# RWKV stage: four groups of two heads in one block, the next group's first exponentials inside the scan, masks and spread products moved

## The chip, the cores and the metric

The kernel runs on one core of a Trainium2 chip. The metric is the device time of one execution in microseconds; where several runs were taken, their median. All times of single instructions come from one profiled execution.

The engines are named as in the profile: PE is TensorE (matmul), PEld its weight load, DVE is VectorE, ACT is ScalarE, POOL is GpSimd, and SP issues the DMAs and clears semaphores.

## The reference

One layer of a hybrid network on 1024 image tokens and 128 prompt tokens (1152 columns in all): an adaptive RMS norm and a half-step SwiGLU, a mixer, another half-step SwiGLU and a last norm. The mixer has a Fourier half and a half of eight RWKV-7 heads of size 64, read forward and backward. What concerns us is the RWKV half:

```python
def step(state, inp):
    r_t, w_t, k_t, v_t, kk_t, a_t = inp
    sa = jnp.einsum('bhvk,bhk->bhv', state, -kk_t)
    state = (state * w_t[:, :, None, :]
             + sa[..., None] * (kk_t * a_t)[:, :, None, :]
             + v_t[..., None] * k_t[:, :, None, :])
    return state, jnp.einsum('bhvk,bhk->bhv', state, r_t)
...
decay = jnp.exp(-jnp.exp(-jax.nn.softplus(-w_raw) - 0.5))
...
y_gn = ((y_sum - mean) * lax.rsqrt(var + GN_EPS)) * ln_w + ln_b
y_rwkv = (y_gn + (bonuses[0] + bonuses[1])) * gate
```

The step runs over all tokens for each head and direction; `y_gn` normalises over the 64 channels of a head, and `gate` is a small product with `gate_g2`.

## The kernel before

The program is a row of stages: load, modulation, first SwiGLU, input projection, Fourier, RWKV, output projection, second SwiGLU, final norm. A stage is a `Stage` object: it owns semaphores (`st.sem(...)`), runs one block in which each engine has its own program, and on leaving it runs one more block in which SP clears every semaphore of the stage, one instruction for each (`for s in self.sems: sp.sem_clear(s)`). All engines meet at the end of a block.

The RWKV part (`rwkv`) works on four groups of two heads. `rw_first` prepares group 0; then there is one stage per group (`rw_pair`: group 0, a hardware loop over groups 1 and 2, group 3); `rw_last` finishes the output of group 3. Both directions (d = 0 and 1) of a group are done together. The tokens are cut in 18 chunks of 64.

A group has two halves. The first one is the chunk algebra, all chunks at once:

- ACT makes two exponentials of each direction (`P0`, `iP0`, `P1`, `iP1`, lines 1979 and 1980; tiles `rw.e1`, `rw.e2`, which lie in the buffer `rw.gr`). DVE scales the operands with them (`pc`, `first`, `A`, `B`, `K`, `R`, lines 1802 to 1818). Ahead of these DVE adds the two directions' outputs of the group in front (`y`, line 1885; its second operand lies in `rw.work`).
- PE works through the list `jobs`, written out by hand; job n uses PSUM bank n % 8 and waits until job n-8 has been copied out. The names are `n` (the matrices to invert), `g` (twelve products, masked by DVE with `masked`, line 1832), `v` and `b` (transposes), `s` (states), `a`, `z`, `f`, `w`, `q`, `x`, `u`, `y`.
- The 16 x 16 diagonal blocks of `n` are inverted by DVE: ACT copies `n` to SBUF, SP sends it to DRAM (line 1532) and fetches its blocks back into lanes (line 1537, 8 DMAs for each direction), DVE does 15 elimination steps of two instructions each (`invert`, lines 1850 and 1853; semaphore steps `times` and `minus`), transposes them (`turn`, line 1857), and SP sends blocks back (lines 1542 and 1545, 8 DMAs each) and loads the whole matrices (`xt`, line 1548, and `x`, line 1550). Jobs `f` wait for `xt`.
- `share = [0, 3, 7, 11, 15]` tells where the masks of `g` jobs 8 to 11 stand between the elimination steps of direction 0: after 3, 7, 11 and 15 of them.
- In groups 1 to 3 (`done`) the norm of the group in front is woven in: jobs `mean`, `var`, `rstd` (the products that spread the reciprocal over the columns, line 1160, which wait for DVE's `inv` and `wide`, lines 1924 and 1167) and `gate`. `rstd` stands ahead of the `u` jobs of direction 0; on DVE `rstd` stands ahead of `rk0` and of the odd `u` jobs.

The second half is the scan, 18 steps. A step is two products on PE for each direction (`S`, line 1710, and `M`, line 1718) with a DVE instruction behind each (lines 1956 and 1965), and the output product `Y` (lines 1730 and 1735) of the step in front, which ACT copies out (line 2020). In groups 0 to 2 (`more`) the preparation of the next group (`Prep`) fills the gaps of the steps; its last instructions are three scans on DVE (line 1308). Preparation of `sw[0]`, which `P0` and `iP0` read, ends in step 11 of the scan.

Of the kernel before, what the change touches and what calls it, by code (L numbers as in the profile page):

```python
# [8 lines left out]
ALU = mybir.AluOpType  # L9
ACT = mybir.ActivationFunctionType  # L10
# [87 lines left out]
class Stage:  # L98


    def __init__(self, nc):
        self.nc, self.sems, self.ctx = nc, [], ExitStack()

    def sem(self, name):
        s = self.ctx.enter_context(self.nc.semaphore(name))
        self.sems.append(s)
        return s
# [988 lines left out]
class Rwkv:  # L1096
# [9 lines left out]
    def __init__(self, nc, ctx):  # L1106
# [31 lines left out]
        self.e1, self.e2 = [[g[:, n * T:(n + 1) * T] for n in (m, m + 1)] for m in (4, 6)]  # L1138
# [293 lines left out]
def rw_pair(nc, io, sb, rw, zd, md, nd, ud, utd, p, done, more):  # L1432
# [6 lines left out]

    GC, NU = 3, 6  # L1440
# [30 lines left out]
    jobs += post("var", 1) + many("g", 1, 6, 10) + many("x", 0, 0, NB) + many("g", 1, 10, G1) + post("rstd", NC)  # L1471
    jobs += many("u", 0, 0, 2 * NB) + many("f", 1, 0, NB) + many("z", 1, 0, NB) + many("y", 0, 0, NB) + post("gate", NC)
# [7 lines left out]
    share = [(BI - 1) * n // 4 for n in range(5)]  # L1480
# [3 lines left out]
    dve_names = ["y"] * done + ["pc0", "first0", "A0", "B0", "pc1", "first1", "A1", "B1", "K0", "R0"]  # L1484
# [3 lines left out]
    dve_names += ["t0"] + inv_of(1, 0, BI - 1) + ["t1", "K1", "R1"]  # L1488
    dve_names += names("mean", 0, 0, NC * done) + names("g", 1, 0, 2) + names("w", 0, 0, NB) + names("g", 1, 2, 6)
    dve_names += names("var", 0, 0, done) + names("g", 1, 6, 10) + names("x", 0, 0, NB) + names("g", 1, 10, G1)  # L1490
    dve_names += ["inv", "wide"] * done + names("rstd", 0, 0, NC * done) + ["rk0"] + odd(0) + names("bonus", 0, 0, NC * done)
# [5 lines left out]
    act_names += act_of("b", 1) + act_of("a", 1) + act_of("q", 1) + act_of("u", 1) + act_of("y", 1)  # L1497
    with Stage(nc) as st, nc.psum_tensor(fresh("g_ps"), [P, 8, 512], F32) as ps:
        pe_t = Steps(st.sem("pe_s"), [name(*job) for job in jobs])
        dve_t = Steps(st.sem("dve_s"), dve_names)  # L1500
        act_t = Steps(st.sem("act_s"), act_names)
        pool_t = Steps(st.sem("pool_s"), ["zero", "one"])
        n_out, n_in, u_out, u_in, t_out, t_in = ([st.sem(f"{n}{d}") for d in range(2)]
                                                 for n in ("n_out", "n_in", "u_out", "u_in", "t_out", "t_in"))
        y_out, s_in, g_in, out_s = st.sem("y_out"), st.sem("s_in"), st.sem("g_in"), st.sem("out_s")
        bank = {job: n % 8 for n, job in enumerate(jobs)}

        spe_t = Steps(st.sem("spe_s"), [x for i in range(NCH) for x in (f"S{i}_0", f"S{i}_1", *[f"Y{i - 1}"] * (i > 0), f"M{i}",
                                                                  *["st"] * (i == NPC + 1))] + [f"Y{NCH - 1}"])
        sdve_t = Steps(st.sem("sdve_s"), ["zero"] + [x for i in range(NCH) for x in  # L1510
                                                     [f"S{i}_0", f"S{i}_1"] + [f"M{i}_0", f"M{i}_1"]])
        sact_t = Steps(st.sem("sact_s"), [x for i in range(NCH) for x in [f"Y{i}"] + ["st"] * (i == NPC)])
        spool_t = Steps(st.sem("spool_s"), [f"mp{i}_{d}" for i, d in SD])
        prep = Prep(st, io, sb, rw, zd, p + 1, ps[:, 6:8, :]) if more else None

        def copied(eng, k, d, n):
            if on_act(k, d, n):
                act_t.wait(eng, name(k, d, n))
            if on_dve(k, d, n):
                dve_t.wait(eng, name(k, d, n))  # L1520

        with st.block() as block:
            @block.sync
            def _(sp):
                flat = lambda t, d: t[d][0:P * T].rearrange("(p t) -> p t", t=T)
                lanes = lambda t, h, b: t[(2 * h + b // 2) * NCH:(2 * h + b // 2 + 1) * NCH, b % 2]
                blocks = lambda t, h, b: diagonal(t, h)[b].rearrange("i c j -> c i j")
                HB = [(h, b) for h in range(2) for b in range(HS // BI)]

                def there(d):  # L1530
                    act_t.wait(sp, name("n", d, NB - 1))
                    sp.dma_start(flat(nd, d), work[:, d * T:(d + 1) * T]).then_inc(n_out[d], 16)
                    sp.wait_ge(n_out[d], 16)
                    if done:
                        dve_t.wait(sp, "y")
                    for h, b in HB:
                        sp.dma_start(lanes(ni[d], h, b), blocks(nd[d], h, b)).then_inc(n_in[d], 16)

                def back(d):
                    dve_t.wait(sp, f"minus{d}_{BI - 2}")  # L1540
                    for h, b in HB:
                        sp.dma_start(blocks(ud[d], h, b), lanes(wi[d], h, b)).then_inc(u_out[d], 16)
                    dve_t.wait(sp, f"t{d}")
                    for h, b in HB:
                        sp.dma_start(blocks(utd[d], h, b), lanes(wit[d], h, b)).then_inc(t_out[d], 16)
                    act_t.wait(sp, "iP1")
                    sp.wait_ge(t_out[d], 16 * len(HB))
                    sp.dma_start(xt[d].rearrange("p c n -> p (c n)"), flat(utd, d)).then_inc(t_in[d], 16)
                    sp.wait_ge(u_out[d], 16 * len(HB))
                    sp.dma_start(x[d].rearrange("p c n -> p (c n)"), flat(ud, d)).then_inc(u_in[d], 16)  # L1550

                for d, key in enumerate(("state_fwd", "state_bwd")):
                    sp.dma_start(rw.st[:, d, :], io[key][0, 0, bass.ds(p * 2, 2), :, :].rearrange("h v k -> (h v) k"))\
                      .then_inc(s_in, 16)
                there(0)
                there(1)
                back(0)
                back(1)
                if done:
                    pe_t.wait(sp, name("gate", 0, NC - 1))  # L1560
                sp.dma_start(rw.g2[:, :], io["gate_g2"][0][:, bass.ds(p * P, P)]).then_inc(g_in, 16)
                if done:
                    dve_t.wait(sp, name("gate", 0, NC - 1))
                    sp.dma_start(md[bass.ds(p + (NP - 1), 1), :, :].rearrange("a p t -> p (a t)"), y).then_inc(y_out, 16)
                if more:
                    pe_t.wait(sp, name("x", 1, NB - 1))
                    dve_t.wait(sp, name("rkk", 0, NC - 1))
                    prep.sync(sp)
                    for sem in prep.z_in + prep.w_in:
                        sp.wait_ge(sem, 16)  # L1570
                sact_t.wait(sp, "st")
                for d, key in enumerate(("state_f", "state_b")):
                    sp.dma_start(io[key][0, 0, bass.ds(p * 2, 2), :, :].rearrange("h v k -> (h v) k"), rw.m0[:, d, :])\
                      .then_inc(out_s, 16)
                for d in range(2):
                    sp.wait_ge(t_in[d], 16)
                    sp.wait_ge(u_in[d], 16)
                sp.wait_ge(s_in, 32)
                sp.wait_ge(g_in, 16)
                if done:  # L1580
                    sp.wait_ge(y_out, 16)
                sp.wait_ge(out_s, 32)

            @block.gpsimd
            def _(pool):
                both = work[0:LANES, 2 * T + 1024:2 * T + 2048]
                if done:
                    dve_t.wait(pool, "y")
                pool_t.did("zero", pool.memset(both, 0.0))
                pool_t.wait(pool, "zero")  # L1590
                pool_t.did("one", pool.memset(both.rearrange("p (k i) -> p k i", i=BI * BI)[:, :, ::BI + 1], 1.0))
                if done:
                    dve_t.wait(pool, "inv")
                    dve_t.wait(pool, "wide")
                for i, d in SD:
                    c = order[d][i]
                    if i:
                        sdve_t.wait(pool, f"M{i - 1}_{d}")
                    else:
                        sdve_t.wait(pool, "zero")  # L1600
                    spool_t.did(f"mp{i}_{d}", pool.tensor_scalar(rw.mp[:, d, :], old(i, d), rw.pc[:, d, c:c + 1], None, ALU.mult))

            @block.tensor
            def _(pe):
                def heads(out, q, w, v):

                    for j in range(NU):
                        for h in range(2):
# [4 lines left out]
                def pair(k, d, q, count, one):  # L1613

                    for j in range(count):
                        for h in range(2):
                            ins = one(ps[:, bank[k, d, 2 * q + h], :], rows_of[h], h, q * count + j, j)
                            if j == count - 1:
                                pe_t.did(name(k, d, 2 * q + h), ins)
# [532 lines left out]
```

## Time and profile before

| | |
|---|---|
| median of 3 runs | 3014.56 us (3010.67 to 3015.2) |
| the profiled execution, device time | 2998.61 us |
| its span (first to last instruction) | 2996.8 us |
| PE busy | 2674.4 us (89%) |
| DVE busy | 1360.5 us (45%) |
| ACT busy | 728.4 us (24%) |
| mean granted TensorE clock | 0.925 |
| RWKV groups, start of the first exponential's table load | 1383.38, 1519.15, 1656.54, 1805.13 us |
| first instruction of `rw_last` | 1934.08 us |

The profile's busy times are sums over the span, so they say which engine is loaded, not what a stage waits for. Granted clock 1.0 is 2.4 GHz and 0.5 is 1.2 GHz.

### The profile page before, as it was taken

To read this page: it belongs to the slowest core of one execution; us is meant where nothing else is said; L and a number is where in the kernel's file an instruction comes from. 1 tells how busy PE (TensorE), PEld (TensorE's weight loads), DVE (VectorE), ACT (ScalarE), POOL (GpSimd) and SP (SyncE) were. 2 spreads that over 40 slices of the span, in tenths; PEclk is the share of its full clock that TensorE was granted. 3 is DMA by queue.
4 is the path that set the end of the run, shared out by engine and by line. 5 is a ranking of instruction groups with operands and counts; after the bars stand their busy time and mean duration, and the time that the engine had idled before them with its cause. 6 is when DMAs were issued, how large, how long until landed. Compare 5 with 4: busy or idle time off the path is not lost. (4 is left out here: it accounts for less than half of the span.)

```text
span 2996.8 us, 51466 instructions
## 1 busy us (share of the span) xinstructions
PE 2674.4 (89%) x21152; PEld 2514.1 (84%) x21152; DVE 1360.5 (45%) x2687; ACT 728.4 (24%) x1367; POOL 86.9 (3%) x158
## 2 busy tenths in 40 slices
PE   4589999999999599976979697977899999999995
PEld 2189999999999599944867676777899999999995
DVE  1353333333333766316475757434533333333335
ACT  1141111111111411115444344222411111111112
POOL 0000000000000000000112020200000000000000
PEclk7689999999999799986889788988899999999997
DMA  8611111111110122142121212051111111111101
GB/s 340 262 50 43 42 42 42 42 42 42 42 42 7 29 84 90 50 175 79 50 62 38 62 37 62 12 183 36 50 43 42 42 42 42 42 42 42 42 7 63
DMA packets 213154, 193.64 MB, mean 65 GB/s; under 512 B 63860, under 2 KB 183455, under 8 KB 213023
## 3 DMA queue, kind: packets, MB, share of 16 engines
q1 hardware_dynamic: 212752, 191.65, 19.8%
q8 instruction: 101, 1.65, 0.2%
q14 instruction: 31, 0.25, 0.0%
q10 hardware_dynamic: 270, 0.09, 0.0%
HBM read 159.01 MB, written 32.70 MB: 64 GB/s over the span
## 5 line engine op out<-in xcount | busy, mean ns | idle before, releaser
L128 PE MATMUL ff_ps<-h_hi,ff_wlo 128*128 128x384 f32 x2112 | 711.1, 337 | 7.2 <-ACT ff_s L604 7.2
L129 PE MATMUL ff_ps<-h_lo,ff_whi 128*128 128x384 f32 x2112 | 710.2, 336 | 0.0
L130 PE MATMUL ff_ps<-h_hi,ff_whi 128*128 128x384 f32 x2112 | 709.6, 336 | 0.0
L652 DVE TENSOR_TENSOR ff_s<-ff_ps,ff_s 128x384 f32<-128x384 f32 x132 | 73.6, 557 | 752.2 <-PE ff_ps L130 750.9
L128 PEld LDWEIGHTS ff_ps<-h_hi,ff_wlo 128*128 128x128 f32 x2112 | 400.3, 190 | 7.8 <-ACT ff_s L604 7.8
L129 PEld LDWEIGHTS ff_ps<-h_lo,ff_whi 128*128 128x128 f32 x2112 | 400.0, 189 | 0.0
L130 PEld LDWEIGHTS ff_ps<-h_hi,ff_whi 128*128 128x128 f32 x2112 | 400.0, 189 | 0.0
L130 PE MATMUL ff_ps<-ff_uhi,ff_whi 128*128 128x384 f32 x1056 | 352.7, 334 | 0.0
L128 PE MATMUL ff_ps<-ff_uhi,ff_wlo 128*128 128x384 f32 x1056 | 352.7, 334 | 0.0
L129 PE MATMUL ff_ps<-ff_ulo,ff_whi 128*128 128x384 f32 x1056 | 352.7, 334 | 0.0
L604 ACT ACTIVATE ff_s<-ff_ps 128x384 f32<-128x384 f32 x132 | 65.0, 493 | 740.6 <-PE ff_ps L130 740.5
L608 ACT ACTIVATE ff_uhi<-ff_s 128x384 fp32r<-128x384 f32 x132 | 69.5, 526 | 556.2 <-DVE ff_s L652 556.2
L663 DVE SCALAR_TENSOR_TENSOR x_again<-ff_ps,mod,x_again 128x256 f32<-128x256 f32 (+1 forms) x352 | 171.0, 514 | 72.1 <-PE ff_ps L130 71.4
L663 DVE SCALAR_TENSOR_TENSOR x<-ff_ps,mod,x 128x256 f32<-128x256 f32 (+1 forms) x352 | 170.9, 514 | 72.2 <-PE ff_ps L130 71.5
L128 PEld LDWEIGHTS ff_ps<-ff_uhi,ff_wlo 128*128 128x128 f32 x1056 | 198.2, 188 | 0.0
L129 PEld LDWEIGHTS ff_ps<-ff_ulo,ff_whi 128*128 128x128 f32 x1056 | 198.2, 188 | 0.0
L130 PEld LDWEIGHTS ff_ps<-ff_uhi,ff_whi 128*128 128x128 f32 x1056 | 198.2, 188 | 0.0
L645 DVE TENSOR_TENSOR ff_wlo<-ff_raw,ff_whi 128x1024 fp32r<-128x1024 f32 x132 | 157.5, 1219 | 17.7 <-ACT ff_whi L599 17.5
L128 PE MATMUL pj_ps<-h_hi,pj_wlo 128*128 128x384 f32 x456 | 154.1, 338 | 1.6 <-DVE h_lo L466 1.6
L129 PE MATMUL pj_ps<-h_lo,pj_whi 128*128 128x384 f32 x456 | 153.1, 336 | 0.0
L130 PE MATMUL pj_ps<-h_hi,pj_whi 128*128 128x384 f32 x456 | 153.1, 336 | 0.0
L599 ACT ACTIVATE ff_whi<-ff_raw 128x1024 fp32r<-128x1024 f32 x132 | 131.9, 1044 | 0.0
(287 smaller groups left out, 3247.9 us busy)
## 6 DMA issues: line engine op xcount, KB each, us to landing
md_w<-w_mod SPq DMA_DIRECT2D x9, 4096.0 KB, 24.2
ff_raw<-ffn_w_gate SPq DMA_DIRECT2D x44, 512.0 KB, 4.6
ff_raw<-ffn_w_up SPq DMA_DIRECT2D x44, 512.0 KB, 3.8
ff_raw<-ffn_w_down SPq DMA_DIRECT2D x44, 512.0 KB, 3.7
pj_raw<-w_in SPq DMA_DIRECT2D x19, 512.0 KB, 4.1
z_dram<-pj_zo SPq DMA_DIRECT2D x15, 576.0 KB, 2.9
rw_rkv<-z_dram SPq DMA_DIRECT2D x12, 576.0 KB, 5.9
x_dram<-x SPq DMA_DIRECT2D x1, 4608.0 KB, 22.1
```

What stands on the lines that cost most here:

```text
L128: pe.matmul(out, w_lo, x_hi, start=start, stop=False)
L129: pe.matmul(out, w_hi, x_lo, start=False, stop=False)
L130: return pe.matmul(out, w_hi, x_hi, start=False, stop=stop)
L599: act.activation(w_hi[:, u, :], raw[:, u % RAW, :], ACT.Copy).then_inc(w_hi_s, 1)
L604: act.activation(silu[:, t % 2, :], ps[:, t % 2, 0:CW], ACT.Silu).then_inc(gate_free, 1)
L608: act.activation(hid_hi[:, m, c * CW:(c + 1) * CW], hid[:, t % 2, :], ACT.Copy).then_inc(hid_hi_s, 1)
L645: dve.tensor_tensor(w_lo[:, u, :], raw[:, u % RAW, :], w_hi[:, u, :].bitcast(F32), ALU.subtract)\
L652: dve.tensor_tensor(hid[:, t % 2, :], ps[:, 2 + t % 2, 0:CW], silu[:, t % 2, :], ALU.mult)\
L663: last = dve.scalar_tensor_tensor(xs, ps[:, 4 + n % 4, a:b], sb["mod"][:, (3 * (2 * f) + 2) * KD + o, s:s + 1], xs, ALU.mult, ALU.add)
```

## The change

All four groups now stand in one `Stage` and one block (`rw_pairs`), written out one behind the other without the hardware loop. Each group still has semaphores of its own, so the stage has the semaphores of all four groups. In place of the meeting of all engines, each engine waits for the steps of the group in front that it needs. Three more things move:

- the first direction's exponentials of the next group (`behind.powers(act, 0)`) are issued by ACT ahead of the last scan step's copies; for this `e1[0]` and `e2[0]` now lie in `rw.work`, and `e1[1]`, `e2[1]` in `rw.gr`. DVE's `y` is moved from the head of the group to behind `R0`, and the lanes' DMAs and POOL's two memsets wait for it (in group 0 for `R0`);
- `share = [0, 1, 2, 3, 5]`: the masks of `g` jobs 8 to 11 stand after 1, 2, 3 and 5 elimination steps;
- `rstd` stands behind the six `u` jobs of direction 0 on PE, and behind `rk0` and the odd `u` jobs on DVE.

```diff
-        self.e1, self.e2 = [[g[:, n * T:(n + 1) * T] for n in (m, m + 1)] for m in (4, 6)]
+        self.e1, self.e2 = [[self.work[:, n * T:(n + 1) * T], g[:, m * T:(m + 1) * T]] for n, m in ((3, 4), (4, 5))]
...
-    jobs += post("var", 1) + many("g", 1, 6, 10) + many("x", 0, 0, NB) + many("g", 1, 10, G1) + post("rstd", NC)
-    jobs += many("u", 0, 0, 2 * NB) + many("f", 1, 0, NB) + many("z", 1, 0, NB) + many("y", 0, 0, NB) + post("gate", NC)
+    jobs += post("var", 1) + many("g", 1, 6, 10) + many("x", 0, 0, NB) + many("g", 1, 10, G1)
+    jobs += many("u", 0, 0, 2 * NB) + post("rstd", NC) + many("f", 1, 0, NB) + many("z", 1, 0, NB) + many("y", 0, 0, NB) + post("gate", NC)
...
-    share = [(BI - 1) * n // 4 for n in range(5)]
+    share = [0, 1, 2, 3, 5]
...
-    dve_names = ["y"] * done + ["pc0", "first0", "A0", "B0", "pc1", "first1", "A1", "B1", "K0", "R0"]
+    dve_names = ["pc0", "first0", "A0", "B0", "pc1", "first1", "A1", "B1", "K0", "R0"] + ["y"] * done
...
+            dve_t.wait(sp, "y" if done else "R0")
...
+        if done:
+            front.sact_t.wait(pe, f"Y{NCH - 1}")
+            front.sdve_t.wait(pe, f"M{NCH - 1}_1")
+            front.prep.act_t.wait(pe, f"w1_{NC - 1}")
...
+    def powers(act, d):
+        if done:
+            front.prep.dve_t.wait(act, f"scan{d}_{NC - 1}")
+        act_t.did(f"P{d}", act.activation(rw.e1[d], rw.sw[d], ACT.Exp, scale=-DECAY))
+        act_t.did(f"iP{d}", act.activation(rw.e2[d], rw.sw[d], ACT.Exp, scale=DECAY))
...
+            if more and i + 1 < NCH:
+                prep.act(act, i + 1)
+                if i + 1 == NCH - 1:
+                    behind.powers(act, 0)
...
+def rw_pairs(nc, io, sb, rw, zd, md, nd, ud, utd):
+
     with Stage(nc) as st, nc.psum_tensor(fresh("g_ps"), [P, 8, 512], F32) as ps:
...
+        pairs = [None]
+        for p in range(NP):
+            st.tag = f"_{p}"
+            pairs.append(rw_pair(st, ps, io, sb, rw, zd, md, nd, ud, utd, p, pairs[-1]))
...
-        rw_pair(nc, io, sb, rw, zd, md, nd, ud, utd, 0, False, True)
-        with nc.Fori(1, NP - 1) as p:
-            rw_pair(nc, io, sb, rw, zd, md, nd, ud, utd, p, True, True)
-        rw_pair(nc, io, sb, rw, zd, md, nd, ud, utd, NP - 1, True, False)
+        rw_pairs(nc, io, sb, rw, zd, md, nd, ud, utd)
```

## Rows read from the trace of the kernel before

**Rows 1.** The page, part 1: busy time, share of the span, instructions.

```profile
PE 2674.4 (89%) x21152; PEld 2514.1 (84%) x21152; DVE 1360.5 (45%) x2687; ACT 728.4 (24%) x1367; POOL 86.9 (3%) x158
```

**Rows 2.** Timeline, group 0 to group 1 (start, us, engine, line, out<-in, idle before <-releaser).

```profile
1513.83 0.22 ACT L2020 ACTIVATE rw_work<-g_ps 128x64 f32<-128x64 f32 x1
...
1515.32 0.95 DVE L1308 TENSOR_TENSOR_SCAN rw_wt<-rw_reset,rw_wt 128x384 f32<-128x384 bf16 x1
...
1515.85 0.22 ACT L2020 ACTIVATE rw_work<-g_ps 128x64 f32<-128x64 f32 x1
1519.15 1.28 ACT L1979 ACT_TABLE_LOAD   x1 [3.08 <-PEq L118]
1519.26 1.36 DVE L1885 TENSOR_TENSOR rw_y<-rw_y,rw_work 128x1152 f32<-128x1152 f32 x1 [2.99 <-PEq L118]
...
1520.44 1.16 ACT L1979 ACTIVATE rw_gr<-rw_wt 128x1152 f32<-128x1152 f32 x1
...
1521.64 0.28 DVE L1802 COPY rw_pc<-rw_gr 128x18 f32<-128x18 f32 x1 [1.02 <-ACT rw_gr L1979]
...
1524.47 6.00 PE L1609 MATMUL g_ps<-rw_ar,rw_bk 64*64 64x64 f32 x144 [8.79 <-DVE rw_bk L1815]
```

**Rows 3.** Timeline, the other two group boundaries: table loads; group 2's `n` jobs.

```profile
1656.54 1.28 ACT L1979 ACT_TABLE_LOAD   x1 [3.33 <-PEq L118]
...
1661.87 7.42 PE L1609 MATMUL g_ps<-rw_ar,rw_bk 64*64 64x64 f32 x144 [9.04 <-DVE rw_bk L1815]
...
1805.13 1.28 ACT L1979 ACT_TABLE_LOAD   x1 [2.92 <-PEq L118]
```

**Rows 4.** Timeline, ACT in group 1: a table load straight behind a copy.

```profile
1568.40 0.49 ACT L1975 ACTIVATE rw_wt<-g_ps 128x384 f32<-128x384 f32 x1 [0.21 <-PE g_ps L1609]
1568.91 1.28 ACT L1996 ACT_TABLE_LOAD   x1
```

**Rows 5.** Timeline, last and first instruction around two stage ends: `rw_first`, group 3.

```profile
1379.47 2.65 DVE L1308 TENSOR_TENSOR_SCAN rw_wt<-rw_reset,rw_wt 128x384 f32<-128x384 bf16 x3
1383.38 0.33 SPq L1553 DMA_DIRECT2D rw_st<-state_fwd  x1
...
1931.95 0.22 ACT L2020 ACTIVATE rw_work<-g_ps 128x64 f32<-128x64 f32 x1
1934.08 1.36 DVE L1407 TENSOR_TENSOR rw_y<-rw_y,rw_work 128x1152 f32<-128x1152 f32 x1 [3.16 <-PEq L118]
```

**Rows 6.** Timeline, start of the elimination in groups 1, 2, 3; masks before it.

```profile
1532.35 3.80 DVE L1832 TENSOR_TENSOR rw_gr<-g_ps,cst 128x384 f32<-128x384 f32 x8
...
1536.75 0.20 DVE L1850 TENSOR_TENSOR rw_work<-rw_work 72x30 f32<-72x30 f32 x1 [0.60 <-DMA rw_work<-n_dram]
...
1674.66 0.21 DVE L1850 TENSOR_TENSOR rw_work<-rw_work 72x30 f32<-72x30 f32 x1 [0.54 <-DMA rw_work<-n_dram]
...
1823.36 0.21 DVE L1850 TENSOR_TENSOR rw_work<-rw_work 72x30 f32<-72x30 f32 x1 [1.23 <-DMA rw_work<-n_dram]
```

**Rows 7.** Timeline: group 0's `f`; group 1's last mask, blocks' DMAs, `f`.

```profile
1422.85 3.55 PE L1609 MATMUL g_ps<-rw_wt,rw_bt 64*64 64x64 f32 x72 [3.55 <-DMA rw_wt<-ut_dram]
...
1546.22 0.55 DVE L1832 TENSOR_TENSOR rw_gr<-g_ps,cst 128x384 f32<-128x384 f32 x1
1546.33 3.45 SPq L1542 DMA_DIRECT2D u_dram<-rw_work  x8
...
1559.14 2.31 PE L1609 MATMUL g_ps<-rw_wt,rw_bt 64*64 64x64 f32 x72 [1.28 <-DMA rw_wt<-ut_dram]
```

**Rows 8.** Timeline, group 1: `rstd` on PE.

```profile
1577.27 0.91 PE L1160 MATMUL g_ps<-cst,rw_kk 128*128 128x128 f32 x6 [2.17 <-DVE rw_kk L1167]
```

**Rows 9.** Windows, a stretch of group 2's scan (length, busy PE/PEld/DVE/ACT/POOL, granted clock, DMA).

```profile
1764.00:1768.00 4.00, 4.00 (x37) 2.74 (x36) 1.51 (x6) 0.65 (x3) 1.38 (x3) 0.50 0.07 16
```

**Rows 10.** Timeline, group 2's scan: two `S` steps in a row on DVE.

```profile
1764.93 0.50 DVE L1956 TENSOR_TENSOR rw_sv<-g_ps,rw_gr 64x128 f32<-64x128 f32 x2 [1.28 <-PE g_ps L1710]
...
1768.59 0.50 DVE L1956 TENSOR_TENSOR rw_sv<-g_ps,rw_gr 64x128 f32<-64x128 f32 x2 [1.04 <-PE g_ps L1710]
```

More of the change, by code:

```diff
@@ new lines, in gpsimd @@
+    def gpsimd(pool):
+        both = work[0:LANES, 2 * T + 1024:2 * T + 2048]
+        dve_t.wait(pool, "y" if done else "R0")
+        pool_t.did("zero", pool.memset(both, 0.0))
+        pool_t.wait(pool, "zero")
+        pool_t.did("one", pool.memset(both.rearrange("p (k i) -> p k i", i=BI * BI)[:, :, ::BI + 1], 1.0))
+        if done:
+            dve_t.wait(pool, "inv")
+            dve_t.wait(pool, "wide")
+        for i, d in SD:
+            c = order[d][i]
+            if i:
+                sdve_t.wait(pool, f"M{i - 1}_{d}")
+            else:
+                sdve_t.wait(pool, "zero")
+            spool_t.did(f"mp{i}_{d}", pool.tensor_scalar(rw.mp[:, d, :], old(i, d), rw.pc[:, d, c:c + 1], None, ALU.mult))
@@ L1524, in _ @@
             def _(sp):
[L1525 to L1571, printed above, removed]
@@ L1582, in _ @@
-                sp.wait_ge(out_s, 32)
+                for pair in pairs[1:]:
+                    pair.sync(sp)
             @block.gpsimd
             def _(pool):
[L1586 to L1601, printed above, removed]
+                for pair in pairs[1:]:
+                    pair.gpsimd(pool)
@@ L1603, in _ @@
             @block.tensor
             def _(pe):
-                def heads(out, q, w, v):
-                    for j in range(NU):
-                        for h in range(2):
-                            last = pe.matmul(out[rows_of[h], j * HS:(j + 1) * HS], w(rows_of[h], h, q * NU + j),
-                                             v(rows_of[h], h, q * NU + j), start=True, stop=True)
-                    return last
[L1613 to L1619, printed above, removed]
@@ L1703, in _ @@
-                for job in jobs[-8:]:
-                    copied(pe, *job)
-                def s_part(i, d):
-                    c = order[d][i]
-                    sdve_t.wait(pe, f"M{i - 1}_{d}" if i else "zero")
-                    for h in range(2):
-                        last = pe.matmul(ps[0:HS, 2 * d + h, 0:HS], rw.ar[rows_of[h], d, 0, c * HS:(c + 1) * HS],
-                                         old(i, d)[rows_of[h]], start=True, stop=True)
-                    spe_t.did(f"S{i}_{d}", last)
@@ L1796, in _ @@
+                for pair in pairs[1:]:
+                    pair.tensor(pe)
             @block.vector
             def _(dve):
[L1798 to L1810 removed]
@@ L1981, in _ @@
-                drain("n", 0)
-                drain("n", 1)
-                drain("v", 0)
-                drain("s", 0)
-                drain("b", 0)
-                drain("a", 0)
-                drain("z", 0)
-                drain("f", 0)
-                if done:
-                    for c in range(NC):
-                        dve_t.wait(act, name("mean", 0, c))
-                        act_t.did(name("sq", 0, c), act.activation(cols(rows, c), cols(y, c), ACT.Square))
-                drain("q", 0)
@@ L2005, in _ @@
[L2005 to L2028 removed]
+                for pair, behind in zip(pairs[1:], pairs[2:] + [None]):
+                    pair.scalar(act, behind)
```

870 lines of the change are left out of this document (481 added, 389 removed).

## The prediction

> **What bounds the kernel now.** I read the page first. PE is busy 89% of the span [rows 1], but that is an average: the SwiGLU and projection stages keep it full, and nothing in the change touches them. The RWKV part lies between 1383.38 us (first table load of group 0) and 1934.08 us (first instruction of `rw_last`), 551 us. There I read the timeline at each place that the diff touches, and asked at each what ends last.
>
> At a group boundary nothing runs but the hand-over: ACT's last copy of group 0 ends at 1516.07, DVE's last scan at 1516.27, the next table load starts at 1519.15, `P0` runs from 1520.44 to 1521.60, DVE starts `pc0` at 1521.64 and PE its first `n` job at 1524.47, after 8.79 us without work [rows 2]. So the start of a group is a chain ACT, DVE, PE. Next the elimination of direction 0 waits for the later of two: the eight masks on DVE and the lanes' DMAs. In group 1 the masks end at 1536.15 (1532.35 + 3.80) and the DMAs 0.60 us later; in groups 2 and 3 the DMAs are 0.54 and 1.23 us later than the masks [rows 6]. Then `f` on PE waits for the DMA of `xt`, after 1.28 us without work [rows 7]: the chain there is elimination, blocks' DMAs, `xt`. From `x` of direction 0 on, PE works without pause to the scan but for one place: `rstd` starts 2.17 us after PE fell idle, since DVE makes `wide` behind the masks [rows 8]. The scan is a chain PE-DVE of 2.02 us a step (copies of steps 16 and 17 at 1513.83 and 1515.85, rows 2).
>
> **1. The boundaries (three).** In the new order ACT's table load follows the copies of step 16. Those end at 1514.05 (1513.83 + 0.22), so the load starts 5.10 us earlier than at 1519.15 [rows 2]. In the other two, ACT's work ended at 1653.21 and 1802.21 (load minus idle, rows 3); the copies of step 16 end 2.02 us before that, at 1651.19 and 1800.19, so the gains are 5.35 and 4.94 us. `pc0` of group 1 would start at 1521.64 - 5.10 = 1516.54, just behind DVE's last scan (1516.27), which is next in line. `P0` and `iP0` push the last copies of the scan back by two 1.16 us exponentials and a table load, to about 1518; PE's first `n` job waits for them, but needs `B0` anyway, at 1524.47 - 5.10 = 1519.37: hidden by 1.4 us. `P1` follows them, ends near 1519.1 and is needed by `pc1`, which stands on DVE behind `B0`, so at about the same 1519.37. If that cover goes, the cost is tenths.
>
> The table load is priced by a row: the load at 1568.91 starts 0.02 us after the copy ahead of it ends (1568.40 + 0.49) and takes 1.28 us [rows 4]. The Trainium skill, ScalarE: Activation LUTs, section What ACT_TABLE_LOAD costs, gives about 1.38 us of drain besides for each switch of table. This case's trace shows none of it at that switch. By the page `pc0` would be 1.4 us later at each boundary, and the forecast 4.1 us higher; it is listed as a rival.
>
> **2. `y` behind `R0`.** `y` (1.36 us, rows 2) ran in the shadow of the table load; now it stands on DVE between `R0` and the masks. What queues behind it on DVE is the `n` masks, then the eight `g` masks; SP's lane DMAs and POOL's memsets wait for it too, but the lane DMAs have the copy to DRAM ahead of them, which comes after the first `n` jobs, and POOL's memsets are needed only at the first elimination step. I cost both at nothing. So the masks end, in group 1, at 1536.15 - 5.10 + 1.36 = 1532.41, and the DMAs at 1536.75 - 5.10 = 1531.65: the masks now end last, and the elimination starts 4.34 us earlier. In group 2: masks 1674.12 - 5.35 + 1.36 = 1670.13, against DMAs at 1669.31, gain 4.53. In group 3: 1822.13 - 4.94 + 1.36 = 1818.55 against 1818.42, gain 4.81 [rows 6]. Sum 13.7 us.
>
> **3. `share`.** The sum of DVE's work to the transpose stays. But the fourth mask stood behind the last elimination step (1546.22, rows 7), and SP's block DMAs, which start at 1546.33, wait for that step alone. Now all four masks stand ahead of it, so the DMAs, `xt` and `f` come 0.55 us later (duration of the mask) in all four groups: 2.2 us. I take it in full, since `f` waits for `xt` in every group. What the earlier masks free (`v`, `b`, `a`, `z`, `mean` on PE and ACT) was not what `f` waited for. It does make PE idle longer before `f`: the last mask comes after 5 elimination steps in place of 15: 9.5 us after the start (1546.22 - 1536.75) up to now, of which three masks are 1.65 us, so a step is 0.52 us; five steps and four masks are an estimated 4.8 us. The 1.28 us of idle time become some 6. There the clock matters: in group 0 `f` came after 3.55 us of idle and took 3.55 us in place of 2.31 [rows 7], 1.24 us more. Group 2's `f` looks like group 0's, group 3's like group 1's. So two groups pay 1.24 us anew: 2.5 us. Bounds: nothing if the clock stays up; and from the `n` jobs, which after 9.04 us of idle took 7.42 us [rows 3] for twice the matmuls of one `f` (2 x 2.31 = 4.62), 2.8 us in each of four groups, of which 2.5 us are paid already: 8.7 us. I take 2.5, because `f` itself is the nearest row.
>
> **4. `rstd` behind `u`.** `u` needs only `x` and `z`, which are there when PE falls idle. PE fills the 2.17 us with it and reaches `rstd` when `wide` is done. Nothing else on PE waits up to the scan, so the scan starts 2.17 us earlier in groups 1 to 3: 6.5 us [rows 8]. On DVE `rstd` comes some 2 us later relative to `wide`; `affine` on ACT comes behind `z` jobs and has over 2 us left. If DVE were late, the `y` jobs' banks would wait; bound: the gain falls to 0.
>
> **5. Semaphore clears.** These aren't in the trace, but stage ends are. `rw_first` has 13 semaphores and takes 1.26 us from its last instruction (1379.47 + 2.65 = 1382.12) to the next stage's first (1383.38); group 3 has 24 (four for the engines, twelve for DMAs named by direction, four more, four for the scan) and takes 1.91 us (1932.17 to 1934.08) [rows 5]. Slope 0.65 / 11 = 0.059 us a semaphore. A group with `Prep` has 32. The one stage of after has 3 x 32 + 24 = 120, and clears them all at its end, ahead of `rw_last`: 96 x 0.059 = 5.7 us more than before. Part 1 counted the three gaps as wholly gone; this part of them is moved to the end. Bounds 0 (if the difference of the two gaps has another cause) and 5.7; I take 5.7.
>
> The loop goes too (its jumps are in the gaps counted), and no engine showed a stall on straight-line code in groups 0 and 3, so written-out code costs nothing.
>
> **Sum:** 13.7 - 2.2 - 2.5 + 6.5 - 5.7 = 9.8 us less. The profiled execution of 2998.61 us (its span and 1.8 us around it) would become 2988.8; the median of the runs shown is 16 us above that execution, and 3014.56 - 9.8 = 3004.8 is the forecast.
>
> **Rivals.**
> - *A slow spell more or less.* In group 2's scan the granted clock is 0.50 over some 16 us [rows 9], and a step takes 1768.59 - 1764.93 = 3.66 us [rows 10] in place of 2.02: 1.64 us for each of some 4.4 steps, 7 us. Group 0's scan has such a spell too, group 1's none. The change shifts when each scan starts. One spell more: 3011.8; one or two fewer: 2998 to 2991. Sentence apart: the Trainium skill, TensorE: Matmul & The Clock Gate, Part 1, calls the moment of the switch variable from run to run; the trace agrees insofar as the three prepared scans differ with the same code.
> - *The clears are free:* 3014.56 - 15.5 = 2999.1. For it: no row shows a clear.
> - *The exponentials come no earlier than the scan's end,* so the change doesn't do what it says: if ACT could start the load only at 1516.07, 2.02 us are lost at each boundary, 6.1 us: 3010.9. Against it: their input is ready in step 11.
> - *The page's drain at each table switch:* 3 x 1.38 = 4.1 us, 3008.9.
> - *Slower: spells in the scans.* One mechanism: the scans of groups 1 and 3, now starting at another moment, fall to 0.50 too, and one of the others twice. Slower by more than 6 us needs 9.8 + 6 = 15.8 us, from the third further spell on (21 us): 3025.8. Against it: group 3 has no preparation and no spell.
>
> **How the numbers follow.** Forecast 0.50, with its own range 2999 to 3010 (`f` clock from nothing to 8.7, part 4 partly lost). One or two spells fewer 0.17, free clears 0.08, one spell more 0.10, late exponentials 0.07, the page's drain 0.03, slower 0.05. Over 2992 to 3012 lie all but two spells fewer and the slower case, and the edges of the forecast. A measurement tells 0.2%, 6 us, from no change: faster is below 3008.5. To faster go 0.45 of the forecast's 0.50, fewer spells and free clears, and little of the drain: 0.71. Within 0.2%: the rest of the forecast, late exponentials, most of one spell more and of the drain: 0.22. Slower: 0.07 with some of one spell more.
>
> **What would show it.** Right: from the last scan instruction to the first `n` matmul of groups 1 to 3 some 3.7 us of PE idle time in place of 8.8; the first elimination step ready behind the masks with no wait for the DMA; no idle before `u`, and `rstd` without a wait; a gap near 7.6 us before `rw_last` in place of 1.9; `f` at 3.55 us in each group. Wrong: a drain ahead of `P0`'s table load, `rw_last` starting without the longer gap, or another count of stretches at 0.50 in the scans, which alone could double or cancel the gain.

## The result, and the profile after

The changed kernel takes 2986.9 us in the median of 20 runs (2976.9 to 3004.6), the kernel before 3008.9 in 20 runs beside it (2992.1 to 3024.6): ratio 0.9943, 95% interval 0.9927 to 0.996, 17 us less by the ratio, 19.5 ± 5.5 by the means (here and below ± is two standard errors of a difference of means). The forecast was 3004.8 with a range from 2992 to 3012. The kernel became faster, as held likeliest, but by about twice the 9.8 us, and its time lies below the range.

The profiled execution of each is a poor witness for this: 3001.67 us after (span 2999.9), 2998.61 before. Both kernels scatter with a standard deviation of nearly 9 us, and this execution of after was one of its slowest. So its rows tell which mechanisms came, not what they were worth in sum.

The page's busy row answers to [rows 1]; PE is 6 us busier, though it does the same 21152 matmuls:

```profile
PE 2680.2 (89%) x21152; PEld 2524.5 (84%) x21152; DVE 1359.8 (45%) x2687; ACT 725.3 (24%) x1367; POOL 86.7 (3%) x158
```

The timeline of after, group 0 to group 1, answers to [rows 2]:

```profile
1518.12 0.22 ACT L2033 ACTIVATE rw_work<-g_ps 128x64 f32<-128x64 f32 x1
1518.36 1.28 ACT L1981 ACT_TABLE_LOAD   x1
...
1519.52 0.45 PE L1737 MATMUL g_ps<-rw_gr,rw_sv 128*64 128x64 f32 x8
...
1520.94 0.18 DVE L1805 COPY rw_pc<-rw_work 128x18 f32<-128x18 f32 x1 [0.39 <-ACT rw_work L1981]
...
1523.87 7.16 PE L1607 MATMUL g_ps<-rw_ar,rw_bk 64*64 64x64 f32 x144 [3.90 <-DVE rw_pc L1805]
```

The table load starts 0.02 us behind the copy of step 16, with no drain. The last `Y` runs a microsecond after it, and PE's idle time ahead of `n` is 3.90 us, where it was 8.79. This is the forecast's first step, within 0.2 us (3.7 us was named). The first elimination step follows the masks without a wait in groups 1 and 2, as forecast; in group 3 of this execution it waited 2.41 us for the lanes' DMAs.

The end of the block answers to [rows 5] (timeline of after, last copy of group 3 and first instruction of `rw_last`):

```profile
1931.96 0.22 ACT L2033 ACTIVATE rw_work<-g_ps 128x64 f32<-128x64 f32 x1
1940.01 1.36 DVE L1408 TENSOR_TENSOR rw_y<-rw_y,rw_work 128x1152 f32<-128x1152 f32 x1 [9.08 <-PEq L119]
```

The gap is 7.83 us, where it was 1.91: the clears, 5.9 us more (forecast 5.7).

`f` and `rstd` of group 1 answer to [rows 7] and [rows 8]; with them the windows ahead of `f` (stretch, length, PE busy with its count, granted clock, DMA share, GB/s):

```profile
1559.22 4.10 PE L1607 MATMUL g_ps<-rw_wt,rw_bt 64*64 64x64 f32 x72 [9.71 <-DMA rw_wt<-ut_dram]
...
1577.29 2.31 PE L1639 MATMUL g_ps<-rw_work,rw_wt 64*64 64x64 f32 x72
...
1579.53 2.27 PE L1161 MATMUL g_ps<-cst,rw_kk 128*128 128x128 f32 x18
```

```profile
1548.00:1552.00 4.00, 1.52 (x5) 1.00 0.36 42
1552.00:1556.00 4.00, 0.00 (x0) 0.73 0.25 28
1556.00:1560.00 4.00, 0.78 (x15) 0.50 0.91 298
1560.00:1564.00 4.00, 4.00 (x69) 0.50 0.50 50
```

`rstd` stands behind `u`, and neither waits, as forecast. PE is idle for 9.71 us ahead of `f` (some 6 were estimated, 1.28 before); the clock falls in that stretch and is still at 0.50 through `f`, which takes 4.10 us here and 3.53 to 4.11 in the four groups (3.55 were forecast in each).

What the sum didn't have, and named only among its rivals, is in the scans. In the profiled execution of before they held 17, 0, 17 and 0 us at 0.50 in groups 0 to 3; in that of after 31, 27, 17 and 0. The windows of after's group 1 scan, its start and its end:

```profile
1608.00:1612.00 4.00, 3.19 (x65) 1.00 0.87 305
1612.00:1614.00 2.00, 0.00 (x0) 1.00 0.20 70
1614.00:1618.00 4.00, 3.74 (x36) 0.66 0.00 0
1618.00:1622.00 4.00, 4.00 (x40) 0.50 0.02 4
...
1638.00:1642.00 4.00, 4.00 (x39) 0.50 0.00 2
1642.00:1646.00 4.00, 4.00 (x74) 0.93 0.02 4
```

Between 1612 and 1614 PE does nothing; then the clock is at 1.2 GHz until about 1643. What it waits for is in the timeline:

```profile
1614.26 0.91 PE L1241 MATMUL g_ps<-rw_lora,rw_a 64*128 64x384 f32 x2 [2.28 <-DMA rw_a<-iclr_a]
```

That is the next group's weight `rw_a`, which `Prep.sync` loads behind the three `rw_rkv` tensors. This row became the key to the experiments.

### The profile page after: what moved, and what is told of

It is laid out like the page before. It is cut to its first block and busy times, and to the rows that moved or that the text cites. A ratio compares the mean times of both kernels' runs of the same rounds, so it can differ in the third digit from the quotient of the medians.

```text
span 2999.9 us, 51344 instructions
## 1 busy us (share of the span) xinstructions
PE 2680.2 (89%) x21152; PEld 2524.5 (84%) x21152; DVE 1359.8 (45%) x2687; ACT 725.3 (24%) x1367; POOL 86.7 (3%) x158
## 3 DMA queue, kind: packets, MB, share of 16 engines
q1 hardware_dynamic: 212752, 191.65, 19.6%
```

## The experiments

### One part at a time, on the kernels as they are

`rstd_alone` and `share_alone` are the kernel before with that part of the diff alone; `one_block_alone` is the changed kernel without these two. `clears_shadow` is the changed kernel with each group's semaphores cleared by SP during the next one:

```diff
             sp.dma_start(md[...], y).then_inc(y_out, 16)
+            act_t.wait(sp, "sqrt")
+            for s in front.sems:
+                sp.sem_clear(s)
+                st.sems.remove(s)
```

> The kernel before, with only the four spread products of rstd and the four DVE multiplications by them moved behind the products u. Theory 1, the sum of the prediction holds part by part and what lies beyond it comes from elsewhere: 2.17 us in each of three groups, so about 6.5 us less than before (2 to 8). Theory 2, the time that the changed kernel gained beyond the sum is in the parts that were priced too low: 10 us less or more. Theory 3, what is given here is taken back behind u, where f and z of the other direction wait: within 2 us of before.

> The kernel before, with only the masks among the elimination steps redistributed (share 0, 1, 2, 3, 5). Theory 1: the blocks land 0.55 us later in four groups and f runs at the slow level in two more, 4.7 us more than before (at least 2 more). Theory 2, the price was wrong in sign: the banks that the masks free let TensorE go on earlier with v, s, b, a and z, and ScalarE with their copies, so that f finds its input sooner; 3 us less or more than that. Theory 3, neither: within 2 us of before.

> The changed kernel with the old order of the spread products and the old share of masks: one block without barriers, exponentials ahead, y behind R0. Theory 1: 5.10 + 5.35 + 4.94 us at the three boundaries less 1.36 x 3 counted within y, in all 13.7 us gained and 5.7 us given back by the clears, 8 us less than before. Theory 2, the block is worth more than its boundaries, because the slow spells of TensorE's clock in the scans fall differently behind it: 14 us less or more, and the excess shows as fewer microseconds at the low level in the scans and in the stretch n to u.

> The changed kernel, with the semaphores of each group cleared by SP during the next group, when every engine has passed its last wait on them, and not all at the end. Theory 1: the gap between the last scan step of group 3 and the closing norm falls from 8.2 to about 2.3 us, and the time by 5.7 us against the changed kernel (about 23 to 25 us less than before, if the changed kernel is 17 to 19 less in this job). Rival: the clears hold SP where it should start a transfer, and part of the 5.7 is lost there: 0 to 3 us against the changed kernel.

| kernel (12 runs each) | ratio to before, 95% | mean against before (35 runs) |
|---|---|---|
| rstd_alone | 0.9981 [0.9956, 1.0006] | -4.5 ± 5.2 us |
| share_alone | 1.0034 [1.001, 1.0059] | +10.1 ± 6.3 |
| one_block_alone | 0.9984 [0.9966, 1.0002] | -7.9 ± 4.0 |
| clears_shadow | 0.9929 [0.9906, 0.9952] | -20.7 ± 5.7 |

The signs are the forecast's, and each size agrees within its error. But the three parts add up to -2.3 us, and together they gave -19.5. With up to 9 us of scatter, as large as the effects, these runs decide nothing more. Only `clears_shadow` shows a thing by itself, in its timeline:

```profile
1916.55 0.22 ACT L2038 ACTIVATE rw_work<-g_ps 128x64 f32<-128x64 f32 x1
1918.69 1.36 DVE L1408 TENSOR_TENSOR rw_y<-rw_y,rw_work 128x1152 f32<-128x1152 f32 x1 [3.17 <-PEq L119]
```

The gap is 1.92 us again, the 1.91 of before: the extra gap was the clears.

### What makes the scatter

In all these profiles the scans have a spell of 17 to 31 us at 1.2 GHz, or none. A prepared scan takes 43.0 us in the kernel before without one, 49.0 with 17 us of it and 54 with 27. The time of an execution goes with it: over the 110 executions of the kernel before beside the experiments, time and mean granted clock correlate with -0.87. Either PE's wait in step 0 starts a spell, or the chain of small products does by itself. Two ways to take the wait away, on both kernels: matmuls whose result nothing reads (`keep_clock`) during the wait,

```diff
             if more and prep.items(i):
+                if i == 0:
+                    keep_clock(pe, sb, ps[:, 0, P:3 * P], 2 * P, 5)
                 prep.pe(pe, i)
```

or `Prep.sync` issuing the loads of `rw_w` and `rw_a` ahead of those of `rw_rkv` (with waits on the latter at the next group's head in the changed kernel).

> The kernel before, with five idle-time matmuls (128x256, results unused) on TensorE in step 0 of the scans of groups 0 to 2, where it waits about 2 us for the weights rw_a. Theory 1, this wait is what lets the clock fall to 1.2 GHz early in the scans, and how long it stays there differs from run to run: the low spells in the scans vanish, the median falls by 12 to 20 us, the scatter over the runs (9 us) by half or more. Rival, the scans' own chains of small products let it fall: spells and scatter stay, the time within 3 us of before.

> The changed kernel with the same five matmuls. Theory 1: no low spells in the scans, scatter halved, and the difference to the filled kernel before is the predicted sum, 9.8 us (7 to 13), because what the change gained beyond it was fewer microseconds at 1.2 GHz. Theory 2, the excess is in the parts themselves (stage boundaries, spread products, masks): the difference of the filled pair stays at 17 to 20 us. Rival as for the filled kernel before: no effect, within 3 us of the changed kernel.

> The kernel before, with the loads of the weights rw_w and rw_a issued ahead of the three loads of rw_rkv instead of behind them. Theory 1: TensorE's wait of about 1.8 to 2.3 us in step 0 goes (5 to 7 us in three groups) and with it the low spells (12 to 20 us): 17 to 27 us less than before, scatter halved. Rival, only the wait goes and the clock falls all the same: 5 to 7 us less. Rival, the later landing of rw_rkv holds ScalarE's rw_kk and what follows by as much: no gain.

> The changed kernel with the weights' loads first. Theory 1: as for the kernel before with its loads first, and 9.8 us (7 to 13) less than that one; about 27 to 37 us less than before in all. Theory 2: 17 to 20 us less than that one.

| kernel | runs, sd | ratio to before, 95% | mean against before (27 runs) |
|---|---|---|---|
| before_filled | 12, 7.1 us | 0.9963 [0.994, 0.9987] | -12.0 ± 5.2 us |
| after_filled | 10, 5.4 | 0.9942 [0.992, 0.9963] | -19.4 ± 4.7 |
| before_loads_first | 12, 4.6 | 0.9958 [0.9937, 0.9978] | -13.7 ± 4.2 |
| after_loads_first | 5, 4.2 | 0.9906 [0.9874, 0.9939] | -30.0 ± 5.0 |

(One further execution of `after_loads_first` took 9078 us and is left out of the mean.) The wait is a cause: without it the kernel before gains 12 to 14 us, and its scatter of 8.3 us falls to 7.1 with the fill and to 4.6 with the loads first. Of the gain with the loads first some 6 us are the waits themselves, as a scan without a spell then takes 41.1 us in place of 43.0.

It isn't the only one, and the traces tell two kinds of spell apart. In the seven profiled kernels that keep the wait (21 prepared scans), the clock falls 3.7 to 6.3 us after the start in 11, with one or two steps begun, and stays low for 27 to 31 us; in 6 it falls 9.9 to 11.0 us after the start, with four steps begun, for 17. The wait is 1.1 to 2.7 us long in 18 of these scans, and under 1 us in three, none of which falls early. Both kinds end in the same place, with eight or nine steps begun, so the earlier fall is the longer spell. In the four profiles without the wait (12 prepared scans) the early kind is gone, and in 4 the clock still falls, 7.3 to 11.4 us after the start; 8 have no spell. The two spells of the kernel before's own profile are of the late kind. At two of the 4 falls without the wait, both in group 0, twelve (`before_loads_first`) and six (`after_filled`) products of only 2 columns stand in a row on PE. Timeline of `before_loads_first`, where the granted clock is 1.00 up to 1468, 0.79 over the next 2 us and then 0.50:

```profile
1468.01 1.70 PE L1152 MATMUL g_ps<-cst,rw_sq 128*128 128x2 f32 x12
...
1469.64 0.58 PE L1710 MATMUL g_ps<-rw_m,rw_ar 64*64 64x64 f32 x5
```

The step behind them runs its first five `S` products in 0.58 us, 0.38 at full clock. The two pairs disagree on the change: 7.5 ± 5.4 us in one, 16.3 ± 4.6 in the other. Theory 1 (9.8) and theory 2 (17 to 20) both survive.

### Scans without spells

So: loads first, and `keep_clock` behind PE's preparation in steps 1 to 3.

```diff
             if more and prep.items(i):
                 prep.pe(pe, i)
+                keep_clock(pe, sb, ps[:, 0, P:3 * P], 2 * P, (0, 1, 2, 1)[i] if i < 4 else 0)
```

`after_f_filled` asks whether the low clock ahead of `f` costs what the forecast said; it puts 16 such matmuls before the wait for `xt`. `everything` has all of these edits and the early clears.

> The kernel before with the weights' loads first and one, two and one idle-time matmuls (128x256) behind TensorE's preparation items in steps 1, 2 and 3 of the scans of groups 0 to 2, where 6 to 12 products of only 2 columns stand in a row. Theory 1, what is left of the low spells in the scans begins there: no scan shows more than 4 us at 1.2 GHz, scatter under 5 us, and the time is that of the kernel before with its loads first (about 14 to 16 less than before) or up to 5 us lower: the four added matmuls of 0.49 us cost up to 6 us in three groups, the spells some 10. Rival, the spells stay as often as they were: 3 to 6 us slower than with the loads first alone.

> The changed kernel with the same two edits. Theory 1, the gain beyond the predicted sum was microseconds at 1.2 GHz in the scans: with the spells gone from both kernels this one is 9.8 us (7 to 13) faster than its partner of this job. Theory 2, the excess is in the parts: 17 to 20 us faster than its partner.

> The changed kernel with 16 idle-time matmuls (128x256, 7.9 us at full clock) ahead of f in all four groups, in the stretch in which TensorE waits 9.7 us for the transposed blocks. Theory 1, with the masks early TensorE runs out of work sooner, the clock falls before f, and the stretch f to u runs 5 to 8 us at 1.2 GHz in each group: it falls from 18.7 us to 16 to 17, 5 to 8 us less in all than the changed kernel. Rival, f to u waits for DVE and ScalarE and not for TensorE: within 2 us of the changed kernel.

> The changed kernel with the semaphores cleared one group late, the weights' loads first, the matmuls in steps 1 to 3 and those ahead of f. If the gains add up: 5.7 + 14 + 5 us less than the changed kernel, some 2965 us and 40 us less than before. If they overlap, 25 to 35 us less than before.

| kernel | runs, sd | ratio to before, 95% | mean |
|---|---|---|---|
| before_scan_filled | 8, 3.2 us | 0.9935 [0.9913, 0.9957] | 2984.0 us |
| after_scan_filled | 6, 1.6 | 0.9891 [0.9865, 0.9917] | 2969.7 |
| after_f_filled | 12, 9.0 | 0.9936 [0.9911, 0.9961] | 2983.6 |
| everything | 6, 5.0 | 0.9878 [0.9849, 0.9906] | 2965.6 |

No scan of the two `scan_filled` profiles has a spell, nor of the seven further profiles with these edits below, and the scatter is a third to a fifth of what it was. Windows of `after_scan_filled` over the start of group 1's scan:

```profile
1600.00:1604.00 4.00, 4.00 (x70) 1.00 0.02 6
1604.00:1608.00 4.00, 3.80 (x54) 1.00 0.00 0
1608.00:1612.00 4.00, 4.00 (x65) 1.00 0.11 24
```

In this pair the change is worth 14.3 us: above the 7 to 13 of theory 1, below the 17 to 20 of theory 2. In `after_f_filled` `f` to `u` takes 50.7 us in groups 1 to 3 together, 55.8 in the changed kernel, as theory 1 had it; but its time, 5.5 ± 6.5 us less, can't confirm it, and in `everything` the same edit brings nothing over `quiet_clears` below (0.3 ± 4.8). The profiles of these two say where the gain goes: `f` to the scan is 6.2 us shorter in the four groups, but elimination to `f` is 1.6 us longer and the scans' ends to the next eliminations 2.5 us.

### The parts on the quiet base

On a base with 3 us of scatter the parts can be sized. The same edits as in the first group, on the `scan_filled` kernels; `base_again` is `before_scan_filled` once more, and `quiet_clears` is `after_scan_filled` with the early clears.

> The kernel before with scans free of low spells (weights' loads first, four matmuls in steps 1 to 3), with only the share of masks changed. Theory 1, as predicted: 4.7 us more than its base (2984 us). Theory 2, the masks early cost only where spread products stand ahead of u: in the stretch f to u some 1.4 us in three groups, nothing between elimination and f: 4 to 5 us more, all of it at f to u. Rival: nothing, because TensorE's lowered clock before f is in both orders: within 1.5 us of the base.

> The same base with only the spread products of rstd and their four DVE multiplications moved behind u. Theory 1: 6.5 us less than the base (5 to 8). Rival: half is taken back behind u: 3 us less.

> The changed kernel with scans free of low spells, with the old share and the old order of the spread products: one block alone. Theory 1: 15.2 us at the three boundaries as the pair of filled kernels shows them, less 5.9 for the clears and 1.4 in group 0, where the elimination's blocks now wait for R0: 8 us less than the base of the kernel before (6 to 10). Rival: the block also shortens what follows, and takes all 14 us of the pair by itself.

> The changed kernel with scans free of low spells and the old share of masks only. Theory 1, the new share costs 4.7 us: this kernel is 4 to 5 us faster than the changed kernel with its scans free of low spells (2969.7 us). Theory 2, within one block the share is free or gains, since TensorE then ends v, b, a and z before the transposed blocks come and starts f at once: the same time or up to 2 us more.

> The changed kernel with scans free of low spells, and with the semaphores of each group cleared during the next one. Theory 1, the 96 clears stand on the path at the end of the block, as the profiles show (8.2 instead of 2.3 us between the last scan and the closing norm): 5.9 us less than the changed kernel with its scans free of low spells (2969.7 us), about 2963.8. Rival, the stages behind take part of it back: less than 3 us.

> The kernel before with scans free of low spells once more, to firm up the base of the comparison (8 runs so far, mean 2984.0 us). If the base holds, 2982 to 2986 us, and the change is worth 14 us without spells; if it was high by chance, 2978 to 2981 us, and the change is worth the predicted 9.8.

| kernel | runs | ratio to before, 95% | mean | against the base, 2984.2 (15 runs) |
|---|---|---|---|---|
| base_again | 7 | 0.993 [0.9905, 0.9956] | 2984.5 us | |
| quiet_share | 12 | 0.9949 [0.9929, 0.9969] | 2989.1 | +4.9 ± 2.2 us |
| quiet_rstd | 6 | 0.9898 [0.9867, 0.9928] | 2974.3 | -9.9 ± 2.3 |
| quiet_block | 6 | 0.989 [0.9859, 0.9921] | 2973.1 | -11.1 ± 2.6 |
| quiet_block_rstd | 6 | 0.9875 [0.9844, 0.9905] | 2968.0 | -16.3 ± 2.4 |
| all three (after_scan_filled) | 6 | above | 2969.7 | -14.5 ± 2.0 |
| quiet_clears | 6 | 0.9869 [0.9839, 0.9898] | 2965.3 | -18.9 ± 3.0 |

(The base is the 15 runs of both its labels. Means are compared over three sessions on two chips; those of the kernel before itself in them, 3001.9, 3005.3 and 3004.7 us, agree within their errors.) The base holds. The block alone is worth 3 us more than forecast, the spread products alone 3 more; in the block they bring 5.2 ± 2.8. The share costs 4.9 alone, 1.7 ± 2.3 in the full change. Its profile doesn't show where the 4.9 arise: from the first `n` to `rw_last` `quiet_share` takes 538.4 us, as both profiles of the base do. The early clears bring 4.4 ± 2.9 of the 5.9 us seen in the gap.

Why the spread products are worth more than their wait is in the timelines of group 1, first of `base_again`:

```profile
1568.47 0.76 DVE L1167 COPY rw_kk<-rw_mp 128x1152 f32<-128x1152 f32 x1
...
1569.37 3.75 PE L1160 MATMUL g_ps<-cst,rw_kk 128*128 128x128 f32 x18 [2.17 <-DVE rw_kk L1167]
```

and its windows:

```profile
1556.00:1560.00 4.00, 4.00 (x96) 1.00 0.32 61
1560.00:1564.00 4.00, 4.00 (x59) 0.79 0.69 243
1564.00:1568.00 4.00, 3.21 (x64) 0.79 0.02 4
1568.00:1572.00 4.00, 2.63 (x12) 0.64 0.00 0
1572.00:1576.00 4.00, 4.00 (x109) 0.93 0.00 0
```

PE waits 2.17 us, the clock falls for the second time, and the 18 matmuls of `rstd` take 3.75 us. In the changed order they take 2.27 (1579.53 above). So the wait costs 2.17 us and then 1.48 us more, where a fall follows it, as in groups 1 and 2 here and not in group 3. `f` to the scan takes 159.7 us in `base_again` (groups 1 to 3 together), 149.2 in `quiet_rstd`: 10.5 us, for a timed 9.9. In the trace that the prediction read the same wait had no fall behind it in any group (18 matmuls in 2.25 us), and `f` to the scan took 154.9 us; there the move would have been worth 5.7 us, close to the 6.5 forecast. Which of the two an execution shows varies: 154.9 to 159.8 over the five profiles with the parts as before.

## Why the prediction was wrong

First the base. 3004.8 was counted from a median of three runs, 3014.56; over 20 runs the median is 3008.9. That is 5.7 of the 17.9 us by which the forecast was off; the rest is the effect, 22.0 us by the medians (19.5 ± 5.5 by the means) where 9.8 was forecast.

The effect, by the terms of the sum. The profile columns compare `base_again` and `before_scan_filled` (the first two numbers) with `after_scan_filled`:

| term | forecast | stretch in the profiles, us | measured |
|---|---|---|---|
| 1 and 2, boundaries and `y` | -13.7 | scan's end to elimination, groups 1 to 3: 65.6, 65.2 -> 50.0 | -15.3 |
| 3, blocks' DMAs later | +2.2 | elimination to `f`, all groups: 90.1, 90.4 -> 89.1 | -1.1 |
| 3 and 4, `f` slow, `rstd` | +2.5 - 6.5 | `f` to scan, groups 1 to 3: 159.7, 159.8 -> 154.2 | -5.5 |
| 5, clears | +5.7 | last scan to `rw_last`: 2.3 -> 8.2 | +5.9 |
| not foreseen | 0 | group 0, `n` to elimination: 11.8, 11.6 -> 13.0 | +1.3 |
| sum | -9.8 | | -14.7 |

The timed value for the same pair is -14.5 ± 2.0. The profiled executions themselves lie 19.6 us apart. The 4.8 us that the table lacks stand outside the RWKV groups, in stages that the change doesn't touch, where one profile differs from the next by as much: from `rw_last` to the end the twenty profiles take 1058.1 to 1063.1 us.

**Boundaries: right in mechanism, 1.6 us too small.** The load behind the copy of step 16, the 3.90 us of idle time and `y` in front of the masks came as worked out. In after the elimination starts 16.7 us behind the last `Y` at most boundaries, in the profiles of before and its versions with other scans 21.1 to 23.6: from `n` to the elimination alone it took 12.3 to 14.6 us there, since the lanes' DMAs end last and vary. The forecast took the three gaps of one execution, 64.4 us in sum, where later profiles have up to 66.2.

**`share`: the step that failed.** "so the DMAs, `xt` and `f` come 0.55 us later (duration of the mask) in all four groups: 2.2 us" isn't seen. Timelines of group 3, `base_again` and then `after_scan_filled`:

```profile
1811.76 0.20 DVE L1851 TENSOR_TENSOR rw_work<-rw_work 72x30 f32<-72x30 f32 x1 [1.12 <-DMA rw_work<-n_dram]
...
1821.34 3.25 SPq L1542 DMA_DIRECT2D u_dram<-rw_work  x8
...
1833.72 2.31 PE L1609 MATMUL g_ps<-rw_wt,rw_bt 64*64 64x64 f32 x72 [1.65 <-DMA rw_wt<-ut_dram]
```

```profile
1790.40 0.19 DVE L1859 TENSOR_TENSOR rw_work<-rw_work 72x30 f32<-72x30 f32 x1
...
1800.30 3.25 SPq L1547 DMA_DIRECT2D u_dram<-rw_work  x8
...
1812.39 4.11 PE L1611 MATMUL g_ps<-rw_wt,rw_bt 64*64 64x64 f32 x72 [7.60 <-DMA rw_wt<-ut_dram]
```

The blocks' DMAs start 9.90 us after the first elimination step in place of 9.58, so 0.3 us of the 0.55 are there, and so it is in every group. At `f` nothing is left of it: 21.99 us for 21.96 here, and over the four groups elimination to `f` is a microsecond shorter. The DMAs between them vary by up to 2 us from group to group, with or without the edit; what takes the 0.3 us back stays open. The other half, `f` at the low clock, is real and larger than 2.5 us (in these rows 4.11 us for 2.31): with `rstd` behind `u`, `f` to `u` takes 15.9 to 17.5 us a group with the old share and 18.5 to 18.7 with the new (`quiet_block_rstd`, `after_scan_filled`). Yet the whole part costs 1.7 ± 2.3 us in the full change. So the 4.7 us agrees with the time of the part alone (4.9 ± 2.2), though the profile of `quiet_share` shows neither half of it there: elimination to `f` is 0.9 us shorter than in the base and `f` to the scans only half a microsecond longer in all, as a slow `f` ahead of a wait for `rstd` costs little. Where the part stands it was priced some 3 us too high.

**`rstd`: right place, a price too low alone.** The forecast took the wait of 2.17 us and not what the clock can do behind it, which its own trace didn't show. Alone it brings 9.9 where 6.5 was said; with the block 5.2, which isn't told from 6.5.

**Clears: right.** 5.9 for 5.7, in the profile and undone in `clears_shadow`.

**Not foreseen:** group 0's elimination starts 1.3 us later. The timelines show `n` 0.5 us longer and the eight lanes' DMA issues taking 4.20 us in after, 3.28 in `base_again`:

```profile
1393.36 4.20 SPq L1538 DMA_DIRECT2D rw_work<-n_dram  x8
...
1398.89 0.21 DVE L1853 TENSOR_TENSOR rw_work<-rw_work 72x30 f32<-72x30 f32 x1 [1.31 <-DMA rw_work<-n_dram]
```

The new wait for `R0` isn't the cause, as `R0` ends at 1391.08. Nor is it the issues' length alone: in 4 of the 11 profiles with one block they take 3.28 us as before, and the elimination still starts 13.1 to 13.6 us behind the first `n`. What makes the lanes' blocks land later stays open.

**The spells.** The rival "a slow spell more or less" was the right thing to name: it is most of the scatter of both kernels. It was put in as a shift of this change, priced at one or two of 7 us; it is in fact redrawn in every execution, and a spell costs 6 us where it is of the late kind and 11 where it is of the early one. Whether after also has fewer on average isn't shown: 19.5 ± 5.5 us with the spells and 14.5 ± 2.0 without overlap. The mean granted clock rises from 0.926 to 0.931 by the change and from 0.933 to 0.937 on the quiet base, so a few microseconds of this kind may be left in it. Of the other rivals none came: the clears weren't free, the exponentials didn't wait for the scan's end, and group 3's scan kept the clock up.

The best version is the changed kernel with the weights' loads first, the four matmuls in steps 1 to 3 and the early clears (`quiet_clears`): 2965.5 us in the median, ratio 0.9869 [0.9839, 0.9898] to before, 20 to 24 us under the changed kernel (20 by each one's distance from the kernel before of its own session, 24 by the means). `everything` is level with it.

## What to carry to other kernels

Before pricing a change of ten microseconds, look for what makes the kernel scatter by as much: here a single wait of TensorE at the head of a long chain of small products could set the clock for half of the chain, and removing it (a load issued earlier) was worth about as much as the change itself. A wait ahead of TensorE is worth its length plus what the next products lose at the low clock, if it falls. Sizes of single parts should be measured on a version without the scatter, and a forecast counted from many runs, not from three. A part that agrees with its forecast in time alone isn't confirmed until a profile shows it where it was said to be.

## What the runs showed of the hardware

- Prepared scans had 1.1 to 2.7 us of PE idle time in step 0 (in three less), and in 11 of 21 the granted clock then fell to 1.2 GHz for 27 to 31 us, with PE listed as busy nearly throughout; 6 more fell later, for 17 us; whether and when differed between scans of the same code. Five idle-time matmuls in that wait, or loading the weights first, took the early falls away (none in 12); with the loads first and four matmuls in steps 1 to 3 no fall was left (none in 27). The Trainium skill, TensorE: Matmul & The Clock Gate, Part 1, calls the moment of the switch variable from run to run, where it describes the rise to the full clock; the traces here show the same of the falls.
- The table load behind a copy showed no drain at the boundaries: 0.02 us between them, and 0.01 us from the load's end to the exponential. By the rule of the Trainium skill, ScalarE: Activation LUTs, What ACT_TABLE_LOAD costs, it would have been some 1.4 us; the trace differs, and the measurement decides.
- A semaphore cleared by SP costs 0.06 us in series with everything else at the end of a block: 96 of them 5.9 us. In the middle of a block the profile shows no cost; the time came back by 4.4 ± 2.9 us.
- 18 matmuls (128x128) took 2.27 us at 1.00 and 3.75 with part of them at 0.50 (mean granted clock 0.64 in the window around them).
